# Retention's values: units of four row blocks by 512 columns, products of 512 columns

## The reference, cut to what matters

```
k = h @ w_k     512 x 256      q = h[latent] @ w_q   256 x 256
v = h @ w_v     512 x 512      g_d = silu(h[latent] @ w_g_d)   256 x 512, d = forward, backward
A_d = (q_rot @ k_rot.T) * decay_d            o_d = A_d @ v
y  += rmsnorm(o_d) * g_d
```

## Time and profile before

| | |
|---|---|
| median of 3 runs | 2503.99 us (2502.05 to 2506.78) |
| profiled execution | 2504.89 us, its span 2503.1 us |
| TensorE (PE) busy | 2447.1 us, 98% of the span |
| VectorE (DVE), ScalarE (ACT), GpSimd (POOL) busy | 1615.9, 1191.7, 339.7 us |
| mean granted TensorE clock | 0.989 of full speed |
| DMA | 401.64 MB, mean 160 GB/s |

### The profile page before, as it was taken

The page is one execution under the profiler, slowest core; times in us unless marked ns, Lnnn a source line. Parts: engine busy times, 40 slices in busy tenths (PEclk is TensorE's granted clock), DMA queues, the critical chain, the costliest instruction groups (busy, mean ns, idle before and its releaser), DMA issues.

```text
span 2503.1 us, 41957 instructions
## 1 busy us (share of the span) xinstructions
PE 2447.1 (98%) x17861; PEld 2271.0 (91%) x17861; DVE 1615.9 (65%) x2441; ACT 1191.7 (48%) x1960; POOL 339.7 (14%) x377
## 2 busy tenths in 40 slices
PE   8999989999999998999999999999999999999998
PEld 7999889999999997899998768888889999999998
DVE  4777666788888866667776956542433555456753
ACT  5444566544454456555454653531333444345643
POOL 1321000332022110032341001100001001101000
PEclk8999999999999999999999989999999999999999
DMA  7576644576777766348785121323222433334552
GB/s 245 196 236 200 180 150 124 182 239 221 251 250 234 240 161 197 107 152 276 272 262 161 51 64 34 93 93 100 95 92 84 146 101 102 102 102 162 171 190 101
DMA packets 386384, 401.64 MB, mean 160 GB/s; under 512 B 44695, under 2 KB 370611, under 8 KB 385940
## 3 DMA queue, kind: packets, MB, share of 16 engines
q1 hardware_dynamic: 383448, 391.19, 49.2%
q10 hardware_dynamic: 2748, 7.76, 0.9%
HBM read 394.72 MB, written 4.19 MB: 159 GB/s over the span
## 4 chain that ended last, share of the span: by engine, by line
PE 77%; DVE 13%; ACT 4%; DMA 3%; issue 2%; POOL 1%; SPq 1%; DVEq 0%; ACTq 0%; POOLq 0%
PE bank L679 23%; PE bank L680 22%; PE bank L681 22%; DVE rounded L2448 6%; PE bank L687 3%; DVE plain L2433 2%; ACT rounded L1661 2%; PE bank L692 2%; PE bank L1584 2%; DMA plain<-in_w_in 2%; POOL plain L3529 1%; PE bank L1104 1%; DMA plain<-in_ffn_w_gate 1%; PE bank L1134 1%; PE bank L782 0%
## 5 line engine op out<-in xcount | busy, mean ns | idle before, releaser
L679 PE MATMUL bank<-rounded 128*128 128x256 f32 (+1 forms) x3680 | 1109.2, 301 | 8.2 <-DVE rounded L2448 4.1
L680 PE MATMUL bank<-rounded 128*128 128x256 f32 (+1 forms) x3680 | 1092.8, 297 | 0.0
L681 PE MATMUL bank<-rounded 128*128 128x256 f32 (+1 forms) x3680 | 1092.7, 297 | 0.0
L2448 DVE TENSOR_TENSOR rounded<-plain,rounded 128x1024 fp32r<-128x1024 f32 (+1 forms) x630 | 742.7, 1226 | 455.8 <-ACT rounded L1661 455.6
L1661 ACT ACTIVATE rounded<-plain 128x1024 fp32r<-128x1024 f32 (+1 forms) x630 | 616.1, 1032 | 304.2 <-PE bank L681 193.4
L679 PEld LDWEIGHTS bank<-rounded 128*128 128x128 f32 x3680 | 709.5, 193 | 44.8 <-issue 9.3
L680 PEld LDWEIGHTS bank<-rounded 128*128 128x128 f32 x3680 | 709.7, 193 | 16.4
L681 PEld LDWEIGHTS bank<-rounded 128*128 128x128 f32 x3680 | 709.3, 193 | 16.5
L679 PE MATMUL bank<-rounded,rounded 128*128 128x256 f32 (+2 forms) x1472 | 451.2, 307 | 9.2 <-DVE plain L2650 3.2
L680 PE MATMUL bank<-rounded,rounded 128*128 128x256 f32 (+2 forms) x1472 | 449.2, 305 | 0.0
L681 PE MATMUL bank<-rounded,rounded 128*128 128x256 f32 (+2 forms) x1472 | 448.8, 305 | 0.0
(11 more groups left out here) (316 smaller groups left out, 1995.2 us busy)
## 6 DMA issues: line engine op xcount, KB each, us to landing
plain<-in_mlp_w SPq DMA_DIRECT2D x64, 1024.0 KB, 5.3
plain<-in_ada_w SPq DMA_DIRECT2D x48, 1024.0 KB, 5.3
plain<-in_ffn_w_gate SPq DMA_DIRECT2D x44, 1024.0 KB, 5.3
plain<-in_ffn_w_up SPq DMA_DIRECT2D x44, 1024.0 KB, 6.0
plain<-in_ffn_w_down SPq DMA_DIRECT2D x32, 1024.0 KB, 5.4
plain<-in_w_in SPq DMA_DIRECT2D x32, 1024.0 KB, 5.2
plain<-in_od_w_in SPq DMA_DIRECT2D x32, 1024.0 KB, 5.6
plain<-in_ffn_w_down SPq DMA_DIRECT2D x16, 768.0 KB, 5.2
```

Of the source, the lines that this page charges most:

```text
L679: pe.matmul(dst, a[0], b[0], start=first and i == 0, stop=False)
L680: pe.matmul(dst, a[0], b[1], start=False, stop=False)
L681: ins = pe.matmul(dst, a[1], b[0], start=False, stop=last and i == n - 1)
L2448: dve.tensor_tensor(low, raw, top, SUB).then_inc(*done(("lo", m, half)))
```

## The change

A head's two value units are now cut the other way: four row blocks (512 of the 1024 inputs) by all 512 columns of the head, 1 MB as before. TensorE takes four banks ahead of the first product, one per tile of 128 tokens. With the first unit it runs in each bank a chain of 12 matmuls of 512 columns and leaves it open; with the second unit it completes the chains, and marks each tile as it ends. ScalarE does `hi` of the unit three after the first value unit ahead of the copies, copies the four banks one by one, and then does `hi` of the unit three after the second. The outputs wait for the last tile's copy. VectorE's, GpSimd's and the sync engine's programs are unchanged.

```diff
@@ plan_odd
             for half in range(2):
-                self.square(("o", "v", h, half), w, 0, 8, 2048 + h * 512 + half * 256, 256)
+                self.gather(("o", "v", h, half), 4, (w[512 * half:512 * half + 512, 2048 + h * 512:2560 + h * 512], 512))
@@ TensorE, odd
+            bv = [bank(s, "v", h, tile) for tile in range(4)]
             for half in range(2):
                 m = U[s, "v", h, half]
                 ready(m)
-                for t2 in range(2):
-                    b = bank(s, "v", h, half, t2)
-                    for tile in range(2):
-                        tok = (2 * t2 + tile) * 128
-                        ins = product(b[:, tile * 256:tile * 256 + 256],
-                                      [(hx(k, tok, tok + 128), part(m, k, 0, 256)) for k in range(8)])
-                    keys = [("unit", m)] if t2 else []
-                    ins.then_inc(*done((s, "v", h, half, t2), *keys))
+                for tile in range(4):
+                    ins = product(bv[tile][:, :], [(hx(4 * half + k, tile * 128, tile * 128 + 128), part(m, k, 0, 512))
+                                                   for k in range(4)], half == 0, half == 1)
+                    keys = [("unit", m)] if tile == 3 else []
+                    if half or keys:
+                        ins.then_inc(*done(*keys, *([(s, "v", h, tile)] if half else [])))
...
-                    for x in new(at(s, "A", h, d), at(s, "v", h, 1, 1, "s")):
+                    for x in new(at(s, "A", h, d), at(s, "v", h, 3, "s")):
@@ ScalarE, odd
-            for half in range(2):
-                for t2 in range(2):
-                    for x in new(at(s, "v", h, half, t2), at(s, "o", h - 1, 1, 1) if h else None):
-                        act.wait_ge(*x)
-                    act.activation(b_.V[:, 2 * t2:2 * t2 + 2, half * 256:half * 256 + 256],
-                                   grid(M.bank(s, "v", h, half, t2)[:, :], c=2), ACT.Copy, scale=1.0).then_inc(
-                        *done((s, "v", h, half, t2, "s"), ("free", s, "v", h, half, t2)))
-                hi(U[s, "v", h, half] + 3)
+            hi(U[s, "v", h, 0] + 3)
+            for tile in range(4):
+                for x in new(at(s, "v", h, tile), at(s, "o", h - 1, 1, 1) if h else None):
+                    act.wait_ge(*x)
+                act.activation(b_.V[:, tile, :], M.bank(s, "v", h, tile)[:, :], ACT.Copy, scale=1.0).then_inc(
+                    *done((s, "v", h, tile, "s"), ("free", s, "v", h, tile)))
+            hi(U[s, "v", h, 1] + 3)
```

## The result

| | before | after |
|---|---|---|
| median, runs taken side by side, 21 each | 2503.23 us (2497.73 to 2510.05) | 2500.93 us (2488.46 to 2506.55) |
| ratio, 95% interval | | 0.9981 (0.9972 to 0.9990) |
| profiled execution, its span | 2504.89, 2503.1 us | 2496.55, 2494.7 us |
| first scores of head 0 to those of head 1 | 81.84 us | 80.57 us |
| matmuls in the trace | 17861 | 17477 |

The change makes the kernel 0.19% faster, 4.8 us by the ratio, with an interval from 2.5 to 7.0 us. The forecast was -5.15 us. The medians of the two lists of runs lie only 2.3 us apart and their means 3.9 us, so the size of the gain is not known closely from whole runs. The stage itself can be read much more sharply than the time of the kernel: its period repeats from head to head within 0.01 us.

What follows compares the result with a forecast made beforehand. TensorE's own instruction stream bounds the kernel in retention, with almost no waits. The sum is -5.15 us from the value products and nothing else: profiled 2504.89 to 2499.7 us, median 2498.8 us, range 2494.5 to 2503.0 us.

Steps and rivals of the forecast that it cites:

- The price of a matmul: TensorE in retention: each matmul pays its columns plus 13.3 ns, 120.0 ns at 256 columns and 226.6 ns at 512.
- part 1: Retention's value products: 96 matmuls of 512 columns replace 192 of 256, gaining 1.29 us a head, 5.15 us over four.
- A: Value matmuls: wide moving weights cost more, 232.5 ns by the line through the mixer's 408 columns; -2.9 us, 2501.1 us; chance 0.08.
- D: Value matmuls: wider ones hide the fixed cost wholly or partly, under 220 ns; up to -10.2 us, 2494 us; chance 0.05.
- the k row: Head 1's k products in retention, 512 columns with weights stationary: 226.6 ns each, taken as the new value matmuls' price.
- rounding to 32 columns: Second reason for the 512-column price: matmuls cost 32 columns more than their width, if 408 counts as 416.
- Rival B: Value matmuls: fixed cost goes with the columns or shrinks to a ns or two; -0 to -1.0 us, 2503 to 2504 us; chance 0.05.
- Part 2: TensorE's wait for four banks before the first value product: cover 9.5 us, 3.3 us in head 0; cost nothing.
- Part 3: ScalarE's rounding ahead of the value copies: done by V + 12.9 us, before the first tile at V + 13.6; cost nothing.
- Part 4: Chain from last value product to outputs: slack 3.6 us, moves 1.29 us forward with TensorE, distances kept.
- Rival C: Tail chain outgrows its 3.6 us slack; 7.4 us longer stalls TensorE 3.8 us a head, 15.2 us, 2514 us; chance 0.04.
- Part 5: Value unit transfers in retention: still 1 MB, half as many pieces of twice the length; cost nothing.

Runs made afterwards that it cites:

- Experiment 1: Changed kernel with each 512-column value matmul issued as two of 256, same units and banks: 2505.98 us, ratio 1.0002 to the kernel before.
- experiment 2: Changed kernel with value tiles 1 to 3 in matmuls of 408 + 104, 416 + 96 and 384 + 128 columns, tile 0 in 512: 2517.52 us, one run.
- experiment 6: Changed kernel with the rounding of the unit three after the first value unit put back behind ScalarE's four copies: 2499.40 us, ratio 0.9988.
- experiment 5: Changed kernel with twelve more ScalarE copies of each head's last value tile, one after the other: 2525.8 us in one run.
- experiment 4: Changed kernel with extra overwritten matmuls in the first value unit's pass, 36 each of 128x128, 64x512, 64x128 (stationary x moving columns): 2558.13 us, one run.

## Why the prediction was right

- **The price of a matmul and part 1** held: 226.6 ns forecast, 226.9 measured; 1.29 us a head forecast, 1.27 measured; -5.15 us, against 4 x 1.27 = 5.1 us in the trace and 4.8 us (2.5 to 7.0) by the ratio. Rivals A (232.5 ns) and D (under 220 ns) are out by the same rows. Experiment 1 shows that nothing else in the change has a share. The choice of the k row over the line through 408 columns was right; the second reason I gave for it, rounding to 32 columns, was wrong (experiment 2). What carried was that the k products have the same width, and that the orientation doesn't matter.
- **Rival B** would have given 1.0 us at most, 240 ns a matmul. The stream of load and rounded matmul pays 13.3 to 13.6 ns beside its columns at 256 and 512, and about 14 ns at 384. The Trainium skill, page "TensorE: Matmul & The Clock Gate", section "Wait — 56ns, not 53.3ns?", has about 2.5 ns instead; the trace doesn't agree for this stream.
- **Part 2** (banks ahead): no wait of TensorE at the first value product in any head, head 0, for which a cover of 3.3 us was forecast, included.
- **Part 3** (ScalarE's order): the rounding ended before the first tile as forecast, and experiment 6 shows that the order is free within the slack.
- **Part 4** (the tail): slack 3.5 us by experiment 5, 3.6 forecast. Rival C had the right place and point of decision, and too low a price: its 15.2 us for 3.8 us of stall in each head leave out the clock, which made it 5.7 to 6.9 us for 4.05.
- **Part 5** (transfers): the packets fell from 386384 to 382285, the time didn't feel it. Experiment 1 has the longer pieces too, 382288 packets, and the old period.
- **The chances.** The forecast lay at the bound of 0.2%, so faster and same were near even, and the measured -0.19% is within the bound by a hair while its interval excludes no change. The scatter that I took from three runs, 4.7 us from end to end, was well under half of what 21 show, 2497.73 to 2510.05 us. The median after came at 2500.93 us, 2.1 us above the 2498.8 forecast and inside the range. That it was inside is in part luck: in three series of runs the kernel before had medians of 2501.21, 2503.23 and 2505.85 us, a scatter about as large as the change itself.

## What to carry to other kernels

Where TensorE never waits, price a matmul by the distance between starts, at every width that the trace offers, and count instructions: here two matmuls of 256 columns cost 13 ns more than one of 512 (240.0 against 226.9). A split that keeps the moving side at 256 columns costs that little; one that goes to 128 falls onto the weight load, and costs 3% of the kernel here, where the split products were 87 of its 2500 us. Read a gain of a few tenths of a per cent from the period of the stage that was changed, not from the difference of two profiles, and look at the granted clock of the untouched stretches before you own the whole difference.

## What the runs showed of the hardware that I had not expected

- In a row of narrow matmuls with a weight load of 128 x 128 each, one comes every 111 to 112 ns, at 96, 104 and 128 columns alike (only the step behind the first of a row is shorter, 0.06 us in experiment 4); with 64 stationary columns, 128 moving ones come every 60.0 ns.
- 512 columns came every 226.9 ns in the kernel after, but 226 to 232 ns, mostly 229 to 231, where neighbouring chains have other widths (experiments 2 and 4, 230 ns with 64 stationary columns). What these 2 to 4 ns are stays open, as do the 2 ns of 408 and 416 columns, and what the fixed cost is made of.
- In one stretch of the even layer, 1480 to 1490 us, the clock stood at 1.2 GHz in the profile before and at 2.4 GHz in the one after, with the same program; with the shorter differences around it, this moved everything behind it by 3.3 us.
- A stall of 4.05 us in a stage that otherwise keeps TensorE busy brought the lower level of the clock on before it ended, and cost 5.7 to 6.9 us.
